# Memory norm and transposes moved into the first feed-forward layer, the neighbourhood mask added by VectorE, another instruction order in the opening

## What is computed

```python
def first_block(x, ...):
    for layer in range(2):
        xn = rms_norm(x, norm_mix[layer])
        if layer % 2 == 0:
            x = x + even_mixer(xn, ...)   # neighbourhood + latent (MLA) attention
        else:
            x = x + odd_mixer(xn, ...)    # dilated attention
        x = x + sq_relu_mlp(rms_norm(x, norm_mlp[layer]), mlp_w1[layer], mlp_w2[layer])
    return rms_norm(x, norm_final)

def second_block(x, mem, ...):
    mem_n = rmsnorm(mem, mem_norm)        # 256 memory tokens of width 1024
    for l in range(2):
        ...
        x = x + 0.5 * swiglu(...)
        mkv = mem_n @ mem_w_kv[l]         # the only use of mem_n
        ...
```

## Time and profile before

| | us |
|---|---|
| median of three runs (lowest, highest) | 1897.55 (1895.66, 1898.09) |
| the profiled execution, its span | 1895.98, 1894.2 |
| busy in the span: TensorE, VectorE, ScalarE, POOL | 1836.2, 1220.4, 936.0, 276.3 |
| one load of x (512 KB), issue to landing, median | 4.7 |
| one weight load (1 MB), issue to landing, typical | 4.9 to 5.4 |
| half a split of a chunk: ScalarE, VectorE | 1.05, 1.22 |
| memory: four squares, two scalings, rounding of 8 blocks, subtraction of 8 blocks | 2.5, 1.4, 3.4, 3.4 |
| adding a chunk's halves (L1290 or L1294), scaling by rows (L1303), a cross copy of ScalarE (L1031) | 0.7, 0.7, 0.6 |

### The profile page before, as it was taken

How to read it: one execution, slowest core, us unless ns; L and a number is a source line. 1 busy time by engine, 2 the same in 40 slices (tenths; PEclk the granted TensorE clock), 3 DMA queues, 4 the chain that set the end, 5 groups by cost and what they waited for, 6 DMA issues and landing times.

```text
span 1894.2 us, 27815 instructions
## 1 busy us (share of the span) xinstructions
PE 1836.2 (97%) x9809; PEld 1555.7 (82%) x9809; DVE 1220.4 (64%) x1542; ACT 936.0 (49%) x1392; POOL 276.3 (15%) x234
## 2 busy tenths in 40 slices
PE   8799999999999999999999999999999999899998
PEld 6668888888877888888888878888888888678886
DVE  5866655767775665566657756665656656856664
ACT  5355445444356544464545445454544545555453
POOL 2110012211201001210023920012000021010012
PEclk9999999999999999999999999999989999999999
DMA  5515555455421655555555535555535555345553
GB/s 185 186 46 177 178 200 198 172 184 178 178 90 56 197 181 200 190 181 183 186 192 179 198 121 180 188 186 192 166 123 178 196 182 176 111 144 177 178 199 133
DMA packets 214822, 319.46 MB, mean 169 GB/s; under 512 B 5984, under 2 KB 167008, under 8 KB 214496
## 3 DMA queue, kind: packets, MB, share of 16 engines
q1 hardware_dynamic: 213616, 313.45, 49.6%
q0 software_dynamic: 848, 4.85, 0.6%
q10 hardware_dynamic: 288, 0.24, 0.0%
HBM read 317.46 MB, written 1.05 MB: 168 GB/s over the span
## 4 chain that ended last, share of the span: by engine, by line
PE 91%; DVE 5%; ACT 3%; issue 1%; POOL 0%; DVEq 0%; POOLq 0%; ACTq 0%
PE PS L648 26%; PE PS L653 14%; PE PS L654 13%; PE PS L655 13%; PE PS L646 13%; PE PS L642 4%; PE PS L643 2%; PE PS L762 1%; DVE W_lo L1278 1%; PE PS L722 1%; PE PS L780 1%; PE PS L797 1%; ACT U L1102 1%; ACT U L1092 1%; PE PS L906 1%
## 5 line engine op out<-in xcount | busy, mean ns | idle before, releaser
L1278 DVE TENSOR_TENSOR W_lo<-W_raw,W_hi 128x1024 fp32r<-128x1024 f32 x598 | 772.1, 1330 | 284.0 <-ACT W_hi L1018 262.4
L648 PE MATMUL PS<-XN,W_hi 128*128 128x512 f32 x2072 | 738.8, 396 | 0.0
L1018 ACT ACTIVATE W_hi<-W_raw 128x1024 fp32r<-128x1024 f32 x598 | 598.7, 1050 | 171.2 <-PE PS L655 116.8
L646 PE MATMUL PS<-XN,W_lo 128*128 128x256 f32 x2072 | 578.7, 279 | 0.0
L648 PEld LDWEIGHTS PS<-XN,W_hi 128*128 128x128 f32 x2072 | 389.0, 188 | 80.0
L646 PEld LDWEIGHTS PS<-XN,W_lo 128*128 128x128 f32 x2072 | 390.9, 189 | 13.6
L1827 POOL TENSOR_TENSOR SX<-U,SX 128x512 fp32r<-128x512 f32 (+1 forms) x98 | 130.1, 1332 | 1271.2 <-ACT SX L1085 1271.2
L653 PE MATMUL PS<-W_hi,SX 128*128 128x512 f32 x780 | 304.4, 390 | 0.2 <-DVE W_lo L1278 0.2
L654 PE MATMUL PS<-W_lo,SX 128*128 128x512 f32 x780 | 303.5, 389 | 0.0
L655 PE MATMUL PS<-W_hi,SX 128*128 128x512 f32 x780 | 303.3, 389 | 0.0
L1031 ACT ACTIVATE T<-PS 128x512 f32<-128x512 f32 x152 | 91.1, 599 | 426.0 <-PE PS L648 425.9
(11 more groups left out here) (160 smaller groups left out, 1541.2 us busy)
## 6 DMA issues: line engine op xcount, KB each, us to landing
W_raw<-in_ffn_w_gate_up SPq DMA_DIRECT2D x88, 1024.0 KB, 5.1
W_raw<-in_mlp_w SPq DMA_DIRECT2D x64, 1024.0 KB, 5.3
W_raw<-in_ffn_w_down SPq DMA_DIRECT2D x44, 1024.0 KB, 4.9
W_raw<-in_od_w_in SPq DMA_DIRECT2D x36, 1024.0 KB, 4.9
W_raw<-in_a_w_in SPq DMA_DIRECT2D x14, 1024.0 KB, 5.0
W_raw<-in_mem_w_kv SPq DMA_DIRECT2D x8, 1024.0 KB, 5.3
W_raw<-in_w_kvf SPq DMA_DIRECT2D x8, 1024.0 KB, 5.4
W_raw<-in_ev_w_in SPq DMA_DIRECT2D x6, 1024.0 KB, 5.3
```

The source lines that it names most:

```text
L646: mm(bank[:, S:], wT(W_lo, slot, k, fb), xn[:, k, 0, :], start=False, stop=False)
L648: last = mm(bank, wT(W_hi, slot, k, fb), both, start=False, stop=k == KD - 1)
L1018: A(W_hi[:, slot, halves(h)], W_raw[:, slot, halves(h)], ACT.Copy).then_inc(w_hi, 1)
L1278: V.tensor_tensor(W_lo[:, slot, halves(h)], W_raw[:, slot, halves(h)], W_hi[:, slot, halves(h)], ALU.subtract).then_inc(w_lo, 1)
```

## The change

1. The stages `mem_scale` and `mem_turn` leave the opening. The feed-forward layer is cut into stages of 2, 2, 2, 2, 2 and 6 chunks; between them stand the squares of the memory's two halves, its scaling and its transposes in two groups of eight. Memory and its scaled copy get buffers of their own (`MEM`, `MEM_S`); its load is issued by POOL after `ev_o`.
2. POOL loads `na_bias` and the later constants in the opening, once the second weight chunk has landed. The mask is added by VectorE, in two halves of 128 x 1536, before and behind the key copies of `mla_k`.
3. Five warm-up products instead of seven. ScalarE makes a tiny Square as soon as the warm-up tile is set, before it waits for the inputs. ScalarE splits both halves of the second chunk before it squares x.
4. The row scales are spread in the first `na_qk` chunk (chunk 2) instead of chunk 1.

```diff
@@ -141,13 +141,11 @@
     natural("latent", w["ev_w_in"], 1536, 1, ncols=416, dest="latent")
-    p.add("mem_scale", "mem_scale")
     p.add("mla_in", "mla_in")
...
     p.add("mla_turn", "mla_turn")
-    p.add("mem_turn", "mem_turn", gain=GAINS["mem"])
-    up("na_qk", w["ev_w_in"], 512, 1, post="copy", dest="na_qk", at=1024, memory=True)
+    up("na_qk", w["ev_w_in"], 512, 1, post="copy", dest="na_qk", at=1024)
     down("ukv", w["ev_w_ukv"], 128, ks=1, after="kv", src="c")
@@ -156,7 +154,14 @@
     norm("mlp0", rows=False, factor="square")
-    up("mlp_up", w["mlp_w1"][0], 0, FF1 // TCOLS, post="relu2", dest="h")
+    mem_steps = [("mem_scale", dict(t=0)), ("mem_scale", dict(t=1)), ("mem_rows", {})] + [
+        ("mem_turn", dict(blocks=b, gain=GAINS["mem"])) for b in ((0, 1), (2, 3))]
+    done = 0
+    for chunks, step in zip((2, 2, 2, 2, 2, 6), mem_steps + [None]):
+        up("mlp_up", w["mlp_w1"][0], done * TCOLS, chunks, post="relu2", dest="h", at=done * 512)
+        done += chunks
+        if step:
+            p.add(step[0], step[0], **step[1])
     down("mlp_down", w["mlp_w2"][0], FF1, factor=True)
@@ -260,8 +265,9 @@
                  c=9792, mla_v=10560, mla_qT=11584, mla_kT=13632, na_bias=15680,
-                 sm=18752, pt=20800, mem=20800, kpe=22848)
-        MEM = region(R["mem"], 2 * D).rearrange("p (t n) -> p t n", t=TT)
+                 sm=18752, pt=20800, kpe=22848)
+        MEM = region(16384, 2 * D).rearrange("p (t n) -> p t n", t=TT)
+        MEM_S = region(18432, 2 * D).rearrange("p (t n) -> p t n", t=TT)
         KPE = region(R["kpe"], TT * 32)
@@ -410,7 +416,7 @@
                 st["i"] = n_norm - st.get("again", False)
-                if not st.get("again"):
+                if not st.get("again") and st.get("t") != 0:
                     n_norm += 2 if st.get("twice") else 1
@@ -427,7 +433,8 @@
             after["led"] = st["lone"]
-            after["raised"] = (st["kind"] == "norm" and st["rows"] and not st["twice"]) or st["kind"] == "fill"
+            after["raised"] = (st["kind"] == "norm" and st["rows"] and not st["twice"]
+                               and st is not stages[0]) or st["kind"] == "fill" or after.get("latents", False)
@@ -477,7 +484,7 @@
                 st["turn"] = k_turn
-                k_turn += 1
+                k_turn += st.get("blocks") != (0, 1)
             if st["kind"] == "norm":
@@ -818,12 +825,11 @@
-            def turn_memory():
+            def turn_memory(blocks):
                 pe.wait_ge(n_scaled, 2)
-                pe.wait_ge(h_done, 3)
-                for b in range(4):
-                    turn_rows(XS, b)
+                for b in blocks:
+                    turn_rows(MEM_S, b)
@@ -837,7 +843,7 @@
             pe.wait_ge(warm, 1)
-            for _ in range(7):
+            for _ in range(5):
                 mm(PS[:, 0, :], T[:, 0:P], T[:, 0:512], start=True, stop=True)
@@ -862,14 +868,14 @@
                     fill_chunk(st)
+                elif kind == "mem_turn":
+                    turn_memory(st["blocks"])
                 elif kind in ("up", "glu"):
...
                             between, at = opens and (lambda: open_attention(opens)), (0, 4)
-                            if st.get("memory"):
-                                between = turn_memory
-                            if st["raised"] and starts(i, s - 1):
+                            if st["raised"] and starts(i, s - 1 if n > 1 else 0):
                                 between, at = (lambda: spread(st)), (1, 0)
@@ -956,8 +962,6 @@
                     if n == 1:
-                        if st["name"] == "ukv":
-                            pe.wait_ge(xm_done, 4)
                         if st["name"] == "uq":
@@ -1037,7 +1041,7 @@
                     act.wait_ge(x_in[t], 16)
-                src = MEM if st["kind"] == "mem_scale" else X
+                src, junk = (MEM, MEM_S) if st["kind"] == "mem_scale" else (X, XS)
                 for b in range(2):
@@ -1045,7 +1049,7 @@
-                    A(XS[:, t, n], src[:, t, n], ACT.Square, scale=D ** -0.5,
+                    A(junk[:, t, n], src[:, t, n], ACT.Square, scale=D ** -0.5,
                       accum_out=ST[:, 2 * t + b:2 * t + b + 1]).then_inc(n_sq, 1)
@@ -1101,9 +1105,10 @@
-            mem_scale = next(st for st in stages if st["kind"] == "mem_scale")
             act.dma_start(K[:, 0:FIRST], a["const"][:, 0:FIRST]).then_inc(first_in, 16)
             act.dma_start(G[:], a["gains"]).then_inc(first_in, 16)
+            act.wait_ge(warm, 1)
+            A(ST[:, 60:61], T[:, 0:1], ACT.Square)
             act.wait_ge(first_in, 32)
@@ -1124,15 +1129,15 @@
                             split_hi(0, 0)
-                            square(st, 0)
                         else:
...
                         if g0 == 0:
-                            split_hi(1, 1, (0,))
+                            split_hi(1, 1)
+                            square(st, 0)
                     if not st["again"]:
                         square(st, 1)
-                    if st["lone"]:
+                    if st["lone"] and g0:
                         split_hi(g0 + 1, slots[1], (1,))
@@ -1141,8 +1146,10 @@
                     cross(g0, u0, pairs[0])
+                elif kind == "mem_scale":
+                    square(st, st["t"])
                 elif kind == "mem_turn":
-                    round_xs(st, XM, 4, range(4))
+                    round_xs(st, XM, 4, st["blocks"])
                 elif kind in ("up", "conv", "natural"):
@@ -1153,15 +1160,12 @@
                                 ahead(g0 + 2 * i + s, slots[s])
-                            if st["raised"] and starts(i, s - 1):
+                            if st["raised"] and starts(i, s - 1 if n > 1 else 0):
                                 keep_rows(st)
...
                                 cross(g0 + 2 * i + s, u0 + 2 * i + s, pairs[s], st.get("times", 1.0))
-                            if st.get("dest") == "latent" and s == 0:
-                                for t in range(TT):
-                                    square(mem_scale, t)
                     early = st.get("next_down")
@@ -1327,7 +1331,7 @@
                     if (e["bias"], e["h"]) == ("na", 0):
-                        dve.wait_ge(bias_ready, 1)
+                        dve.wait_ge(bias_ready, 2)
                     for t in range(TT):
@@ -1415,6 +1419,15 @@
+            def window_bias(hs):
+
+                dve.wait_ge(bias_in, 16)
+                rows = len(hs) * SLOTS
+                view = region(R["na_bias"] + hs[0] * SLOTS * GRID, rows * GRID).rearrange(
+                    "p (r n) -> p r n", r=rows)
+                V.tensor_tensor(view, view, const("window").unsqueeze(1).to_broadcast([P, rows, GRID]),
+                                ALU.add).then_inc(bias_ready, 1)
+
@@ -1430,11 +1443,13 @@
                     rows_at = st["n_rows"]
-                if kind == "mem_scale":
+                if kind == "mem_rows":
                     for t in range(TT):
-                        dve.wait_ge(n_rstd, 2 * st["i"] + t + 1)
-                        V.tensor_scalar(XS[:, t, :], MEM[:, t, :], ST[:, 2 * t:2 * t + 1], None,
+                        dve.wait_ge(n_rstd, 2 * mem_i + t + 1)
+                        V.tensor_scalar(MEM_S[:, t, :], MEM[:, t, :], ST[:, 2 * t:2 * t + 1], None,
                                         ALU.mult).then_inc(n_scaled, 1)
+                elif kind == "mem_scale":
+                    mem_i = st["i"]
                 elif kind == "final":
@@ -1470,7 +1485,7 @@
                 elif kind == "mem_turn":
-                    for b in range(4):
+                    for b in st["blocks"]:
                         rest_xs(st, XM, 4 + b, b).then_inc(xm_done, 1)
@@ -1678,11 +1693,13 @@
                 elif kind == "mla_k":
+                    window_bias(range(0, 4))
                     for b in range(2):
...
                                       .rearrange("p b n -> p (b n)")).then_inc(acc_read, 1)
+                    window_bias(range(4, 8))
                 elif kind == "forget":
@@ -1763,8 +1780,9 @@
                                     ALU.mult)
-            pool.wait_ge(x_in[1], 16)
-            pool.dma_start(MEM, a["mem_2"][0].rearrange("(t p) n -> p t n", p=P)).then_inc(mem_in, 16)
+            pool.wait_ge(raw_full[1], 16)
+            pool.dma_start(region(R["na_bias"], NA_H * SLOTS * GRID), a["na_bias"]).then_inc(bias_in, 16)
+            pool.dma_start(K[:, FIRST:], a["const"][:, FIRST:]).then_inc(consts_in, 16)
             for st in stages:
@@ -1775,7 +1793,7 @@
                 if kind in ("final", "mem_scale"):
-                    for t in range(TT):
+                    for t in range(TT) if kind == "final" else (st["t"],):
                         mean(st["i"], t)
@@ -1807,18 +1825,6 @@
                     rstd(ST[:, 6:8], 128, mla_r)
-                if st["name"] == "na_v":
-
-                    bias = region(R["na_bias"], NA_H * SLOTS * GRID)
```

(13 more changed lines are left out.)

## The result

The changed kernel takes 1886.79 us (median of five, 1884.94 to 1891.32) against 1897.55 for the kernel before: ratio 0.995, 95% interval 0.9935 to 0.9966. The profiled execution took 1887.32, its span 1885.5. Six more executions on another occasion gave 1888.74. The forecast was 1889.7, in a range of 1884.5 to 1893.5.

The account below looks back on a forecast made before the run. TensorE, busy 1836.2 of 1894.2 us, was taken as the bound, so only its work and waits count; -4.0 - 5.7 + 1.9 = -7.8 from 1897.55 gives 1889.7, range 1887 to 1892, with A down to 1884.5, up to 1893.5.

Parts of the forecast that it names:

- Opening, what goes: Before the first product: shorter warm-up -1.72 and moved table load -1.28 us, first product at 11.85, low-clock stretch stays.
- Opening, what takes its place: Third chunk: its weights wait for POOL's load, landing at 23.0; TensorE idles 2.9 us, spending the opening's 3.0.
- Both bounds: Landing of the third chunk's load: 18.3 if not delayed by POOL's load, 23.4 if strictly behind it.
- Rival A: Early load does not hold the third chunk's weights up: -12.1 us in all, 1885.5; chance 0.27.
- The fifth chunk and after: Without the memory work there, the chunk after ukv starts at 49.2 instead of 53.26: -4.0 us.
- The mask: Mask on VectorE, before the first scores: rope wait of 4.0 falls to about 0.15, transposes at full clock: -5.7 us.
- the 0.9 + 0.9 + 0.2 us: Clock credit within the mask's -5.7: head transposes 0.9, next products 0.9, where first scores' results are awaited 0.2 us.
- Memory in the feed-forward layer: Sixteen transposes added to TensorE there: +1.9 us; squares 2.5 and rounding 3.4 us on ScalarE covered by products.
- Sum: Whole kernel: -4.0 - 5.7 + 1.9 = -7.8 us, giving 1889.7; chance 0.53.
- B: Mask becomes VectorE's bottleneck at POOL's price, rope and split slip by 3.4 us: -2.8 in all, 1894.8; chance 0.10.
- C: Memory steps don't fit, ScalarE's 5.9 us lie open at the layer's stage ends: 1895.6; chance 0.05.
- D: Early load starves the weights longer; slower than before if third chunk lands past 30.8, up to 1904.2; chance 0.05.

Follow-up runs that it names:

- late_load: Changed kernel with POOL's mask load issued at about 30 us and the constants at the last projection, instead of both at 11 us; 1882.14 us, ratio 0.9932.
- late_again: The same kernel as late_load, run once more on another chip; 1885.92 us, ratio 0.9937.
- mask_before: Kernel before with the mask part alone: two halves on VectorE, mask loaded at about 30 us, constants at the last projection; 1891.61 us, ratio 0.9973.
- mem_only: Kernel before with only the memory norm and transposes moved into the first feed-forward layer; 1892.42 us over 12 executions, ratio 0.9983.

## Why the prediction was right, point by point

- **Opening, what goes.** First product forecast 11.85, measured 11.89, with an idle time of 2.62. The table load ran at 1.67, as said, and the low stretch stayed (the products at 12.4 take 0.55 each). That the first product came within 0.04 us is luck. In the eight other profiles with five warm-up calls it came between 12.10 and 13.43, because the warm-up took 6.3 to 7.6 us there and 6.07 here; with seven calls it took 7.7 to 8.2 in five profiles. By the medians of the two groups the warm-up lost 1.0 us and not the 1.72 of the prediction, and the first product came 2.3 us earlier (15.03 to 12.71) and not 3.0. The prediction took the two calls from the fast ones. More of the remaining ones were slow in the other profiles: their median duration is 0.59 us here, 0.90 in late_load and 1.06 in late_again.
- **Opening, what takes its place.** Landing forecast 23.0, measured 24.0; idle forecast 2.9, measured 3.93. Both bounds had been drawn at 18.3 and 23.4, so the measurement is 0.6 past my upper end: POOL's load was issued 0.3 later (10.92 for 10.6) and was through at 20.8 instead of 20.1. Rival A (the load does not hold the weights up) would have been the case with a late load, and late_load shows its third chunk at 23.44.
- **The fifth chunk and after.** Forecast -4.0, measured -2.3 (50.94). This is the term that was mis-sized. VectorE's addition for the fourth chunk came at 41.5 instead of 39.5: 1.0 of it is the landing, 1.0 the low clock after the wait, counted at 1.6 us and in fact 2.7 (0.50 over the first 3.6 us of the chunk, 0.82 over the next five). The chain behind it gave 0.3 back. The stop for L1677 went, as said, and `ukv` waits 1.12 for W_lo. The second profile of the changed kernel lacks the 1.0 of the clock: its low stretch behind the wait (2.85 us there, the landing at 23.7) cost about 1.6, the addition came at 40.3, and the chunk behind `ukv` began at 49.78, -3.5. So the mis-sizing that both profiles show is 0.5 us, and the rest is where the low clock fell.
- **The mask.** Forecast -5.7 between that chunk and the first scores, measured -5.8 (25.8 us instead of 31.6), but the sum is made of other terms. The second mask was said to cost 0.1; it cost 1.48. I had put it beside products at the low clock that followed the 2.2 us wait in the kernel before; in the changed kernel the same wait of 2.24 was followed by full clock:

```profile
54.00:66.00 12.00, 8.86 (x56) 7.52 (x54) 11.16 (x12) 4.29 (x6) 1.27 (x1) 1.00 0.46 158
```

  So TensorE came about 1.6 us sooner to the last projection and waited there; the two cancel. late_again shows it from the other side: there the clock fell after that wait, and the 1.5 us are missing. Counted to the norm behind the attention the part kept its 5.9 us in the changed kernel (93.6 us before, 87.7 and 87.8 in two profiles). In the profiled execution of mask_before it was worth 2.8 there, because low stretches came up inside the attention: the 0.9 + 0.9 + 0.2 us that I credited to the clock were not safe.
- **Memory in the feed-forward layer.** Forecast +1.9, measured +1.7 in the changed kernel (both profiles) and in mem_only. Squares 2.5 us as said, rounding 3.1 for 3.4, no wait of TensorE.
- **Sum.** Forecast -7.8; the profiled spans differ by 8.7, of which 2.1 are not the change's. So the change itself made 6.6 in that pair. The mean over all executions fell from 1896.2 to 1888.3, by 7.9, of which 4.8 are at full clock and 3.2 are less loss to the clock. The second profile's span is 7.7 below that of the kernel before, with the marks at -9.3 (norm ahead of the layer, forecast -9.7), +1.7 (layer) and -7.6 (last norm). That the sum came this close is in part luck all the same: the opening's 3.0 us were forecast 0.7 too good and did not count, and the second mask's wait and the faster products ahead of it cancelled.
- **Rivals.** B (POOL's price for the mask) did not happen, VectorE took 1.75. C did not happen. D's mechanism, the early load starving the weights, is real, but the load landed at 24.0, far from the 30.8 at which the sign would have turned.

The parts at full clock are memory -1.9, mask -2.7 to -2.9, opening -2.2 where no early load takes it back, early load +3.0. They add up to -3.8 to -4.0, against -4.8 (standard error 0.4) for the whole. With the parts' own errors of 0.5 to 0.8 this is no contradiction; the moved squares, splits and row scales, which no run tests alone, may hold some of the difference.

## What to carry to other kernels

Moving a large load early is not free because the queue looks idle: ask which transfer is issued next on another queue, and whether its reader will be ready before it has landed. Here 2.65 MB spent the whole gain of the opening, 1.5 MB at the same place cost nothing that the full-clock times show, and neither did the load 20 us later. When a wait disappears, look at the operation that now stands last on the engine that filled it: moving one half of the mask behind the split that TensorE needs took the remaining 1.5 us. And where single parts are worth 2 us, compare with the loss to the granted clock taken out as well as without, take more than five executions, and look at a second profile before a term is called right or wrong. A low-clock stretch that an edit removes may only move.

## What the runs showed of the hardware that was not expected

- **Two queues share packet by packet, and bytes by packet size.** From 17.5 to 18 us POOL's queue moved 24 packets and SyncE's 23, but 0.19 against 0.02 MB. The Trainium skill (DMA: Bandwidth & Descriptors, Queues, rings and completion order) says that an engine takes turns between queues, a packet at a time. The trace agrees from 17 us on. Before that it differs: the weight load was issued at 13.00, and up to 16.5 us no packet of it moved (one of 1 MB alone has landed 5.3 us after its issue). In the prediction I held the weights to be strictly behind; the time is nearly the same either way, since 0.13 MB of 1 MB got through by 20.0 us, when most of POOL's rows had passed.
- **The same wait is not always followed by the same clock.** After 2.24 us of idleness the granted clock fell to 0.54 in the kernel before, stayed at 1.00 in the changed kernel and in late_load, and fell again in late_again and mask_before, whose transposes right behind that wait take 1.86 and 1.80 us for eight instead of 1.08. A credit for a clock that "will not fall" after a shorter wait is therefore not safe.
- **The loss to the clock varies from execution to execution** of one kernel by several microseconds: 13.2 to 20.8 us over eleven of the changed kernel. Summed over windows of 5 us, the low stretches of the fourteen profiles before 1870 us cost about 1.7 us or a multiple of it each; what differs between the profiles is how many there are, and where.
- **A POOL load late is harmless where its neighbour was issued first.** In late_load the mask was issued at 30.31 and took 7.0 us; the load of `ukv` issued just before it took its 3.6 us and the next weight chunk, issued six microseconds later, 5.4.
